# A two-block network on one core: conditioning weights by column blocks, four v tiles beside their load, later conditioning units spread

## The chip, the cores and the metric

The kernel runs on one core of a Trainium2 chip. The metric is the time of one execution on the device in microseconds; of several executions the median counts. The engines are TensorE (PE in the profile; PEld is its loading of stationary operands), VectorE (DVE), ScalarE (ACT), GpSimd (POOL) and SyncE (SP, which here only issues loads of weights).

## What is computed

Two blocks on 256 tokens of width D = 2048. The first has two layers, and each is steered by a conditioning vector: `mod = silu(cond) @ ada_w + ada_b`, three parts of 2048 each (shift, scale, gate).

```python
sh, sc, g = ada_params(c, ada_w[layer], ada_b[layer])     # latent; for the context with c_ctx
xm = x * (1.0 + sc) + sh
q, k, v, o, z_m, gates, u_p, z_p = split(xm @ w_in)       # layer 0, latent and context
x  = layer_norm(ALPHA * x + g * (y @ w_out), ln_g, ln_b)
```

Layer 0 is an mLSTM in both directions beside a pooling branch; it needs shift and scale for the latent and the context input, and k, v and gates for both. Layer 1 is a gated spatial mixer (u1, v1, z1) for the latent input alone. The second block (attention, a linear recurrence, an expert network) takes the rest of the time, and nothing of it is touched. `ada_w` has 2 x 3 parts of 2048 x 2048 float32.

## The kernel before

All weights come in **units** of 128 x 2048 float32 (1 MB) through a ring of RING = 4 slots in SBUF, in the order of the table STAGES: a name, a pattern of N and P, how often it is repeated, tiles per N unit, and the engine that takes the results out of PSUM. SP issues a load when its slot is free again (L364), strictly in that order.

An **N unit** is 16 weight blocks of 128 x 128. float32 products are made in three products of a faster format (fp32r): ScalarE copies each half of a unit into `unit_hi` (L862, two halves of 1024 columns), GpSimd makes the rest `unit_lo` = ring - unit_hi (L421), and TensorE multiplies hi x hi, hi x lo and lo x hi (L474, `n_unit`). The inputs have a hi and a lo as well. There are NBUF = 4 half-unit buffers: ScalarE may write a half when TensorE is done with the one four halves back (`half_done`), and a slot of the ring is free when `lo_done` says that both rests are made. A unit with one input set has 48 products of 256 columns, one with latent and context (gates, k, v) 96. Results go to four tiles of PSUM in turn; a tile is free again when `tile_free` has been counted up by VectorE or ScalarE.

A **P unit** is used as it is. `ada_ss`, 32 of them at the start, are rows of `ada_w` for shift and scale of layer 0: TensorE takes `cond` (128 x 2) as stationary operand and multiplies 4 x 512 columns per unit in plain float32 (L535), for all 16 parts of the contraction, so that no column is done before the last unit. Then the two rows are copied out (L1303, L930), turned into columns by 32 small products (L542), `mod` is made, VectorE makes the modulated inputs (L1314), ScalarE their hi (L883), GpSimd and VectorE their lo (L406, L1218), and gates can begin. The other 64 P units (gate of layer 0; shift, scale, gate of layer 1) are needed for one row only: VectorE multiplies each by its entry of `cond` and adds it to `ada_acc`, 128 x 2048 (`ada`, L1164). After each 16 of them TensorE sums over the partitions by 16 products of one column (`ada_sum`, L484). These P units stand among the N units: 16 in v, 16 in k, 4 each in q, o, zm and up, 16 in out0.

In v every result is copied to `vstage`, transposed (L554) and copied to `v` by VectorE (`v_step`, `v_out`). Between these steps VectorE does the chain of the gates (`log1p`, L1230 to L1238, and scans). In out0 and out1 VectorE adds each tile to the residual (L1549) and to `h_acc` (L1272); in v1 it copies it and adds it to `h_acc`.

## Time and profile before

| | us |
|---|---|
| median of 3 executions | 4313.85 (4307.5 to 4319.14) |
| the profiled execution | 4325.57 |
| its span, first to last instruction | 4323.8 |
| PE busy | 3878.8 (90%) |
| POOL busy | 3107.3 (72%) |
| DVE busy | 1800.1 (42%) |
| ACT busy | 1612.5 (37%) |

Busy times overlap. TensorE's records are pipelined, so its busy time is an upper bound of its work. The chain of work that ended last consists of PE for 73% of the span, DVE for 13%, POOL for 5% and time of issue for 6%. Its largest lines are L474 (49%) and L838 in the expert network (17%). All weights together are 671 loads of 1 MB.

### The profile page before, as it was taken

How to read it: one execution, taken by the hardware profiler on the slowest of the kernel's cores; microseconds unless marked ns; L12 is line 12 of the kernel's file. 1: busy time of each engine (PE TensorE's matmuls, PEld its weight loads, DVE VectorE, ACT ScalarE, POOL GpSimd, SP SyncE). 2: the span in 40 equal slices, each digit the busy share in tenths (PEclk: the TensorE clock that was granted, in tenths of full speed). 3: DMA queues.
4: the chain of work that ended last, by engine and by line, in shares of the span. 5: the costliest groups of instructions: out<-in, count | busy, mean ns of one | idle time of the engine just before them, and what ended most of it. 6: DMA issues, size and time to landing. Idle time of an engine off the chain costs nothing.

```text
span 4323.8 us, 78214 instructions
## 1 busy us (share of the span) xinstructions
PE 3878.8 (90%) x31142; PEld 3695.3 (85%) x31142; DVE 1800.1 (42%) x2279; ACT 1612.5 (37%) x2283; POOL 3107.3 (72%) x1292
## 2 busy tenths in 40 slices
PE   9699996879998889989998999948999999399987
PEld 1599995779997779989998999938999999399986
DVE  0667357845123351381133492194442000944433
ACT  0112432233343333354433344454443444544442
POOL 0357970867785647778887798878887888888864
PEclk9799997989998999999999999959999999599998
DMA  8367650734443323444444444504454544045532
GB/s 348 122 247 263 263 195 0 269 137 158 166 176 112 129 106 146 156 160 181 177 176 159 180 175 184 185 10 156 184 185 174 184 184 175 0 175 185 186 136 98
DMA packets 98367, 713.79 MB, mean 165 GB/s; under 512 B 11040, under 2 KB 11168, under 8 KB 12064
## 3 DMA queue, kind: packets, MB, share of 16 engines
q1 hardware_dynamic: 97344, 705.75, 43.7%
q10 hardware_dynamic: 864, 5.76, 0.4%
q8 instruction: 119, 1.95, 0.2%
q14 instruction: 40, 0.33, 0.0%
HBM read 709.37 MB, written 2.10 MB: 165 GB/s over the span
## 4 chain that ended last, share of the span: by engine, by line
PE 73%; DVE 13%; issue 6%; POOL 5%; ACT 2%; DMA 1%; DVEq 0%; POOLq 0%; ACTq 0%; SPq 0%
PE bank L474 49%; PE bank L838 17%; POOL unit_lo L421 5%; PE bank L535 2%; DVE hot L1856 1%; PE bank L521 1%; DMA ring<-in_w 1%; DVE peer_w L1870 1%; DVE log_a L1747 1%; DVE hot L1863 1%; DVE rms_tmp L1612 1%; PE bank L627 1%; PE bank L609 0%; DVE y_attn L1733 0%; ACT att_s L1010 0%
## 5 line engine op out<-in xcount | busy, mean ns | idle before, releaser
L421 POOL TENSOR_TENSOR unit_lo<-ring,unit_hi 128x1024 fp32r<-128x1024 f32 x1140 | 2867.9, 2532 | 872.2 <-ACT unit_hi L862 871.0
L474 PE MATMUL bank<-xl_hi,unit_hi 128*128 128x256 f32 x5696 | 1614.3, 283 | 144.0 <-POOL unit_lo L421 58.7
L862 ACT ACTIVATE unit_hi<-ring 128x1024 fp32r<-128x1024 f32 x1140 | 1173.3, 1055 | 1314.8 <-PE bank L474 522.3
L474 PE MATMUL bank<-xl_lo,unit_hi 128*128 128x256 f32 x5696 | 1604.0, 282 | 0.0
L474 PE MATMUL bank<-xl_hi,unit_lo 128*128 128x256 f32 x5696 | 1602.7, 281 | 0.0
L474 PEld LDWEIGHTS bank<-xl_hi,unit_hi 128*128 128x128 f32 x5696 | 1083.4, 190 | 158.6 <-issue 70.9
L474 PEld LDWEIGHTS bank<-xl_lo,unit_hi 128*128 128x128 f32 x5696 | 1082.9, 190 | 0.1
L474 PEld LDWEIGHTS bank<-xl_hi,unit_lo 128*128 128x128 f32 x5696 | 1082.8, 190 | 0.0
L838 PE MATMUL bank<-w_r,unit_hi 128*128 128x256 f32 x4096 | 727.8, 280 | 6.9 <-DVE w_r L1894 6.9
L838 PEld LDWEIGHTS bank<-w_r,unit_hi 128*128 128x128 f32 x4096 | 628.5, 189 | 7.2 <-issue 7.2
L838 PE MATMUL bank<-w_r,unit_lo 128*128 128x256 f32 x2048 | 573.1, 280 | 0.0
L1894 DVE TENSOR_TENSOR w_r<-peer_w,w_r 128x256 fp32r<-128x256 f32 x128 | 294.4, 2300 | 424.3 <-ACT w_r L1103 424.3
L838 PEld LDWEIGHTS bank<-w_r,unit_lo 128*128 128x128 f32 x2048 | 386.0, 188 | 0.0
L1856 DVE TENSOR_TENSOR hot<-con,peer_gT 128x512 bf16<-128x512 f32 x64 | 96.6, 1510 | 434.6 <-ACT hotg L1092 434.6
L1164 DVE SCALAR_TENSOR_TENSOR ada_acc<-ring,cond,ada_acc 128x2048 f32<-128x2048 f32 x64 | 214.5, 3351 | 69.5 <-DMA ring<-in_w 65.5
L439 POOL TENSOR_TENSOR hotg<-hot,gate_parts 128x512 bf16<-128x512 bf16 x128 | 189.2, 1500 | 52.5 <-DVE hot L1856 42.3
L815 PE MATMUL bank<-hotg,hot 128*128 128x64 bf16 x1536 | 91.7, 239 | 143.2 <-POOL hotg L439 136.9
L1079 ACT ACTIVATE peer_w<-bank 128x256 f32 (+1 forms) x128 | 49.3, 385 | 446.3 <-PE bank L474 446.3
L815 PEld LDWEIGHTS bank<-hotg,hot 128*128 128x128 bf16 x1536 | 83.3, 128 | 151.7 <-issue 151.7
L1092 ACT ACTIVATE hotg<-hot,peer_gT 128x64 bf16<-128x64 bf16 x512 | 128.5, 334 | 100.2 <-DVE hot L1856 100.2
L535 PE MATMUL bank<-ring,cond 128*2 128x512 f32 x256 | 112.5, 601 | 7.3 <-DMA ring<-in_w 7.2
L1863 DVE TENSOR_TENSOR hot<-con,peer_gT 128x1024 bf16<-128x1024 f32 x64 | 116.0, 1812 | 0.0
(362 smaller groups left out, 4333.0 us busy)
## 6 DMA issues: line engine op xcount, KB each, us to landing
ring<-in_w SPq DMA_DIRECT2D x671, 1024.0 KB, 4.8
resid<-in_xT ACTq DMA_DIRECT2D x1, 2048.0 KB, 12.8
tmp_ctx<-in_ctxT ACTq DMA_DIRECT2D x1, 2048.0 KB, 10.0
out<-resid SPq DMA_DIRECT2D x4, 512.0 KB, 2.6
con<-in_con ACTq DMA_DIRECT2D x1, 576.0 KB, 3.5
...
```

The source lines that it names most:

```text
L421: pool.tensor_tensor(lb[b][:], ring[slot][:, f * HALF:(f + 1) * HALF], hb[b][:].bitcast(F32), ALU.subtract).then_inc(lo_done, 1)
L439: ins = pool.tensor_tensor(ob[k][:, x], oe[k][:], gb[:, x, bass.ds(it * (2 * TG) + k * TG, TG)].unsqueeze(2) .to_broadcast([P, TG, I2]), A ...
L474: mm = pe.matmul(bank[(s.t0 + tile[m]) % TILES][:, 0:T], w[b][:, (i % 8) * P:(i % 8 + 1) * P], mv[x][:, k, :], start=(k == 0 and w is hb a ...
L535: mm = pe.matmul(bank[4 * (u % 2) + i][0:2, :], cond[:, u // 2, :], ring[u % RING][:, i * 512:(i + 1) * 512], start=(u < 2), stop=(u >= 2 ...
L815: mm = pe.matmul(bank[5 + k][:, t * I2:(t + 1) * I2], oa[k][:, t, :], ob[k][:, x, t, :], start=(x == 0), stop=(x == 2), skip_group_check=True)
L838: mm = pe.matmul(o, w_[b][:, c * P:(c + 1) * P], wr[j % 2][:, x, :], start=(first and j == 0 and cc % 2 == 0 and w_ is hb and x == 0), sto ...
L862: act.activation(hb[b][:], ring[slot][:, f * HALF:(f + 1) * HALF], ACT.Copy).then_inc(hi_done, 1)
L1092: ins = act.activation(ob[k][:, 0, t, :], oe[k][:, t, :], ACT.Copy, scale=gT[:, 2:3, bass.ds(it * (2 * TG) + (k * TG + t), 1)] .rearrange( ...
L1164: dve.scalar_tensor_tensor(a[:], ring[u % RING][:], col, a[:], ALU.mult, ALU.add).then_inc(plain_done, 1)
L1856: dve.tensor_tensor(oe[k][:], bc(C("iota", r * I2, (r + 1) * I2), TG), gT[:, 1, bass.ds(i * TG, TG)].unsqueeze(2).to_broadcast([P, TG, I2] ...
L1863: dve.tensor_tensor(oa[k][:], bc(C("iota"), TG), gT[:, 0, bass.ds(i * TG, TG)].unsqueeze(2) .to_broadcast([P, TG, NKEY]), ALU.is_equal).th ...
L1894: dve.tensor_tensor(wr[j % 2][:, 1, :], at(W, i), wr[j % 2][:, 0, :].bitcast(F32), ALU.subtract).then_inc(S("wr_ready"), 1)
```

## The change

- The load stage is renamed `first` and has 36 units, all N. 32 are A units: 4 parts of the contraction x 512 features of `ada_w`, shift or scale, so that the columns of one block of 512 are done after 8 units (g = 0 to 3). `cond` too is split in hi and lo, side by side as a stationary operand of 4 columns (`cond_parts`): one product with `unit_hi` gives cond_hi x hi and cond_lo x hi in separate rows, one with `unit_lo` gives cond_hi x lo (`ada_unit`). VectorE adds the two pairs of columns when it makes `mod` (`modulated`).
- Behind each g the rows are copied, turned (8 small products, `ada_turn`), and 4 chunks of the modulated inputs are made, hi by ScalarE, lo by VectorE (`x_hi`, `x_lo`).
- 4 are L units: the first four v tiles, one quarter g of the contraction each, for both inputs into four banks (`both_sets`). They stand at places 12, 21, 34 and 35 of the 36.
- In this stage VectorE makes the rests of the units; GpSimd waits until it is over.
- v keeps 4 N units and 8 P. gates go to a bank of their own. The transposes of the v tiles run through v and the first three k units.
- out0 has P after every second N (8 in all, the last two closer), v1 gets 8 P and z1 gets 8. There are six sums in place of four: after v, k, up, within out0, within u1 and after z1. The scale of layer 1 is now in v and out0, the gate of layer 1 in v1 and z1, and parts of `mod` are put together in two steps.

```diff
-    ("ada_ss", "PPPP", 8, 0, "D"),
+    ("first", "N" * 36, 1, 0, "D"),
     ("gates", "N", 1, 2, "D"),
-    ("v", "NPPNPPNPPNPP", 2, 2, "D"),
-    ("k", "NPPNPPNPPNPP", 2, 2, "D"),
+    ("v", "NPP" * 4, 1, 2, "D"),
+    ("k", "NPP" * 8, 1, 2, "D"),
     ("q", "NNPNNPNNPNNP", 1, 1, "D"),
     ("o", "NNPNNPNNPNNP", 1, 1, "A"),
     ("zm", "NNPNNPNNPNNP", 1, 1, "A"),
     ("up", "NNPNNPNNPNNP", 1, 1, "D"),
     ("zp", "NNNN", 2, 1, "A"),
     ("poolw", "P", 1, 0, "D"),
-    ("out0", "NPNPNPNP", 4, 1, "D"),
-    ("v1", "NNNN", 4, 1, "D"),
+    ("out0", "NNP" * 6 + "NPNPNN", 1, 1, "D"),
+    ("v1", "NNPNNPNNPNNP", 2, 1, "D"),
     ("u1", "NNNN", 4, 1, "A"),
     ("wsp", "P", 1, 0, "D"),
-    ("z1", "NNNN", 4, 1, "A"),
+    ("z1", "NNP" * 6 + "NPNPNN", 1, 1, "A"),
...
+FIRST = ([("A", 0, i) for i in range(8)] + [("A", 1, i) for i in range(4)] + [("L", 0, 0)]
+         + [("A", 1, i) for i in range(4, 8)] + [("A", 2, i) for i in range(4)] + [("L", 1, 0)]
+         + [("A", 2, i) for i in range(4, 8)] + [("A", 3, i) for i in range(8)] + [("L", 2, 0), ("L", 3, 0)])
+ENDS = [FIRST.index(("A", g, 7)) for g in range(4)]
...
+            pool.wait_ge(lo_done, 2 * NFIRST)
+            for s in ORDER[1:]:
...
-                pe.wait_ge(plain_done, PLAN["out0"].p0 + KC if b == 3 else 2 * KC + KC * (b + 1))
+                name, n = (("v", 8), ("k", 16), ("up", 4), ("out0", 8), ("v1", 8), ("z1", 8))[b]
+                pe.wait_ge(plain_done, PLAN[name].p0 + n)
+                a = accs.get(name, acc)
...
+            def ada_unit(n, g, i):
+                b = i // 4
+                rows = bank[4 + b]
+                if i % 4 == 0 and g:
+                    pe.wait_ge(S("ada_rows"), 2 * (g - 1) + b + 1)
+                for f in range(2):
+                    u = (2 * n + f) % NBUF
+                    pe.wait_ge(lo_done, 2 * n + f + 1)
+                    for q in range(2):
+                        k = 4 * (i % 4) + 2 * f + q
+                        pe.matmul(rows[0:4, :], ch[:, k, :], hb[u][:, q * 512:(q + 1) * 512],
+                                  start=(k == 0), stop=False, skip_group_check=True)
+                        mm = pe.matmul(rows[0:2, :], ch[:, k, 0:2], lb[u][:, q * 512:(q + 1) * 512],
+                                       start=False, stop=(k == KC - 1), skip_group_check=True)
+                    mm.then_inc(half_done, 1)
+            def ada_turn(g):
+                pe.wait_ge(S("ada_rows"), 2 * g + 2)
+                if g:
+                    pe.wait_ge(S("mod_ready"), g)
+                for b in range(2):
+                    for c in range(GR):
+                        mm = pe.matmul(bank[6][:, 4 * (b * GR + c):4 * (b * GR + c) + 4],
+                                       arow[:, b, c * P:(c + 1) * P], ident[0:4, 0:4],
+                                       start=True, stop=True, skip_group_check=True)
+                mm.then_inc(S("ada_cols"), 1)
...
+            for n, (kind, g, i) in enumerate(FIRST):
+                for gt_ in range(NG):
+                    if n == ENDS[gt_] + (2 if gt_ < 3 else 1):
+                        ada_turn(gt_)
+                if kind == "A":
+                    ada_unit(n, g, i)
+                    continue
+                pe.wait_ge(S("xm_lead"), 2 * g + 2)
+                for f in range(2):
+                    b = (2 * n + f) % NBUF
+                    pe.wait_ge(lo_done, 2 * n + f + 1)
+                    for i in range(8 * f, 8 * f + 8):
+                        mm = both_sets(bank[i % 4], (hb, lb), b, i, (xl, xc), GR * g + i // 4,
+                                       g == 0 and i < 4, g == 3 and i >= 12)
+                    mm.then_inc(half_done, 1)
...
+            v_transposes(0)
+            pe.wait_ge(S("v_lead"), 8)
+            run("v", [xl, xc], extra=lambda it, j: v_transposes(j + 1))
...
+            run("out0", [xl], extra=lambda it, j: ada_sum(3) if j == 14 else None)
             acc_sum(bank[5][:, 0:T], 1, "ln0_sum")
             feature_sum(sq0, bank[6][:, 0:T], "ln0_in", 1, "ln0_sum")
-            ada_sum(3)
...
+            run("u1", [xl], mid=(1, lambda: ada_sum(4)))
...
+            ada_sum(5)
...
+            def modulated(g):
+                dve.wait_ge(S("ada_cols"), g + 1)
+                if g == 0:
+                    dve.wait_ge(S("vec_in"), 16)
+                for b, first, one in ((0, 16, 1.0), (1, 0, 0.0)):
+                    cols = bank[6][:, 16 * b:16 * b + 16].rearrange("p (c s) -> p c s", s=4)
+                    part = mod[:, first + GR * g:first + GR * (g + 1), :]
+                    bias = V("ada_b", first + GR * g, GR).unsqueeze(2).to_broadcast([P, GR, 2])
+                    go(dve.scalar_tensor_tensor(part, cols[:, :, 0:2], one, bias, ALU.add, ALU.add)); sync()
+                    go(dve.tensor_tensor(part, cols[:, :, 2:4], part, ALU.add))
+                event("mod_ready")
+                for x, s, tmp, name in ((h, 0, tl_, "x_in"), (tc_, 1, tc_, "ctx_in")):
+                    if g == 0:
+                        dve.wait_ge(S(name), 16)
+                    for c in range(GR * g, GR * (g + 1)):
+                        go(dve.tensor_scalar(tmp[:, c, :], x[:, c, :], mcol(16 + c, s), mcol(c, s), ALU.mult, ALU.add))
+                    event("xm_tmp")
+            def x_lo(g):
+                for m, (pair, src) in enumerate(((xl, tl_), (xc, tc_))):
+                    lo([group(pair[0], g), group(pair[1], g)], group(src, g), "xm_hi", 2 * g + m + 1, "xm_lead")
+            for n in range(NFIRST + 1):
+                for g in range(NG):
+                    if n == ENDS[g] + (3 if g < 3 else 2):
+                        modulated(g)
+                    if n == ENDS[g] + (5 if g < 3 else 3):
+                        x_lo(g)
+                for f in range(2 if n < NFIRST else 0):
+                    b = (2 * n + f) % NBUF
+                    dve.wait_ge(hi_done, 2 * n + f + 1)
+                    dve.tensor_tensor(lb[b][:], ring[n % RING][:, f * HALF:(f + 1) * HALF], hb[b][:].bitcast(F32),
+                                      ALU.subtract).then_inc(lo_done, 1)
+            dve.wait_ge(half_done, NBUF + 2 * NFIRST)
+            dve.wait_ge(S("xm_lead"), 2 * NG)
...
+            dve.wait_ge(S("ada_sum"), 4)
+            go(dve.tensor_tensor(mod[:, 64:80, 0], bank[4][:, 112:128], mod[:, 64:80, 0], ALU.add)); sync()
+            go(dve.tensor_tensor(mod[:, 64:80, 1], mod[:, 64:80, 0], V("pln_g", 0, KC), ALU.mult))
+            go(dve.tensor_tensor(mod[:, 48:64, 1], mod[:, 64:80, 0], V("pln_b", 0, KC), ALU.mult)); sync()
+            go(dve.tensor_tensor(mod[:, 48:64, 1], mod[:, 48:64, 1], mod[:, 48:64, 0], ALU.add)); sync()
```

The order of VectorE in the load stage, before: behind a wait for all 32 units, the rows are copied (`ada_rows`), `mod` is made (L1307, L1309), and the first four chunks of the latent input follow.

```order
L1303 COPY ada_rows<-bank 2x512 x4
L1307 TENSOR_TENSOR mod<-bank,vec 128x64
L1309 TENSOR_SCALAR mod<-mod 128x32
L1314 TENSOR_SCALAR tmp_lat<-resid,mod 128x256 x4
L1288 MEMSET tick 1x1
L1314 TENSOR_SCALAR tmp_lat<-resid,mod 128x256 x4
```

Now, around the end of the first group of 8 A units: rests of two units, the four small instructions for `mod`, four chunks of each input, and again rests of units (`ring_49` to `ring_52` are the slots of the ring).

```order
L1419 TENSOR_TENSOR unit_lo_59<-ring_50,unit_hi_55 128x1024
L1419 TENSOR_TENSOR unit_lo_60<-ring_50,unit_hi_56 128x1024
L1396 SCALAR_TENSOR_TENSOR mod<-bank,vec 128x8
L1397 TENSOR_TENSOR mod<-bank,mod 128x8
L1396 SCALAR_TENSOR_TENSOR mod<-bank,vec 128x8
L1397 TENSOR_TENSOR mod<-bank,mod 128x8
L1371 MEMSET tick 1x1
L1403 TENSOR_SCALAR tmp_lat<-resid,mod 128x256 x4
L1371 MEMSET tick 1x1
L1403 TENSOR_SCALAR tmp_ctx<-tmp_ctx,mod 128x256 x4
L1371 MEMSET tick 1x1
L1419 TENSOR_TENSOR unit_lo_57<-ring_51,unit_hi_53 128x1024
```

What was one stretch with nothing else on the engine stands now, in four parts, in the stream of the rests for which TensorE waits.

VectorE in out0, before, two N units (the addition into the accumulator, the residual, the sum for LayerNorm):

```order
L1164 SCALAR_TENSOR_TENSOR ada_acc_107<-ring_52,cond,ada_acc_107 128x2048
...
L1549 SCALAR_TENSOR_TENSOR resid<-bank,mod,resid 128x256
...
L1272 TENSOR_TENSOR h_acc<-h_acc,resid 128x256
...
L1164 SCALAR_TENSOR_TENSOR ada_acc_107<-ring_50,cond,ada_acc_107 128x2048
...
L1549 SCALAR_TENSOR_TENSOR resid<-bank,mod,resid 128x256
...
L1272 TENSOR_TENSOR h_acc<-h_acc,resid 128x256
```

Now, three N units:

```order
L1655 SCALAR_TENSOR_TENSOR resid<-bank,mod,resid 128x256
L1355 TENSOR_TENSOR h_acc<-h_acc,resid 128x256
L1247 SCALAR_TENSOR_TENSOR ada_acc_108<-ring_49,cond,ada_acc_108 128x2048
L1655 SCALAR_TENSOR_TENSOR resid<-bank,mod,resid 128x256
L1355 TENSOR_TENSOR h_acc<-h_acc,resid 128x256
L1655 SCALAR_TENSOR_TENSOR resid<-bank,mod,resid 128x256
L1355 TENSOR_TENSOR h_acc<-h_acc,resid 128x256
L1247 SCALAR_TENSOR_TENSOR ada_acc_108<-ring_52,cond,ada_acc_108 128x2048
```

An addition of 128 x 2048 comes before every second unit and no longer before every one.

## Rows read from the trace of the kernel before

**Rows 1.** The page: span, and PEclk over 40 slices of 108 us.

```profile
span 4323.8 us, 78214 instructions
...
PEclk9799997989998999999999999959999999599998
```

**Rows 2.** Windows by stage: length, busy us of each engine (instructions), granted clock, DMA share, GB/s.

```profile
0.00:122.50 122.50, 112.51 (x256) 21.76 (x256) 4.47 (x12) 5.53 (x8) 4.86 (x6) 1.00 0.89 344
122.50:135.20 12.70, 12.66 (x64) 12.60 (x64) 0.00 (x0) 0.00 (x0) 0.00 (x0) 0.55 0.33 129
135.20:161.20 26.00, 0.00 (x0) 0.00 (x0) 23.98 (x43) 11.63 (x11) 13.13 (x5) 0.50 0.00 0
161.20:174.40 13.20, 13.14 (x96) 12.93 (x96) 0.00 (x0) 0.00 (x0) 4.53 (x2) 0.87 0.21 81
174.40:289.00 114.60, 104.42 (x849) 103.89 (x849) 86.83 (x75) 22.41 (x21) 57.63 (x18) 0.93 0.58 221
...
752.20:872.00 119.80, 96.51 (x768) 93.41 (x768) 97.22 (x59) 35.09 (x35) 102.85 (x32) 0.96 0.69 261
...
895.70:1018.90 123.20, 106.86 (x801) 104.08 (x802) 38.61 (x74) 45.58 (x41) 79.04 (x33) 0.91 0.37 137
```

**Rows 3.** Timeline of PE: start, us, instructions, [idle before and what ended it].

```profile
122.54 12.66 PE L542 MATMUL bank<-con,ada_rows 2*128 2x2 f32 x64 [2.73 <-DVE ada_rows L1303]
161.22 0.58 PE L474 MATMUL bank<-xl_hi,unit_hi 128*128 128x256 f32 x1 [26.02 <-DVE xc_lo L1218]
```

**Rows 4.** Lines, 0 to 1330 us: count | busy, mean ns | idle before.

```profile
L421 POOL TENSOR_TENSOR unit_lo<-ring,unit_hi 128x1024 fp32r<-128x1024 f32 x276 | 758.0, 2769 | 364.0 <-ACT unit_hi L862 363.6
...
L862 ACT ACTIVATE unit_hi<-ring 128x1024 fp32r<-128x1024 f32 x276 | 281.6, 1054 | 520.4 <-DMA ring<-in_w 372.7 <-PE bank L474 147.4
L1164 DVE SCALAR_TENSOR_TENSOR ada_acc<-ring,cond,ada_acc 128x2048 f32<-128x2048 f32 x64 | 214.5, 3351 | 69.5 <-DMA ring<-in_w 65.5 <-DVE ada_acc L1164 1.8 <-DVE ada_acc L1172 0.5
...
L484 PE MATMUL bank<-con,ada_acc 128*128 128x1 f32 x128 | 16.8, 265 | 0.0
```

**Rows 5.** Timeline of DVE, single rows from the load stage to v1.

```profile
137.24 1.38 DVE L1314 TENSOR_SCALAR tmp_lat<-resid,mod 128x256 f32<-128x256 f32 x4
...
191.79 0.76 DVE L1348 COPY vstage<-bank 128x256 f32<-128x256 f32 x2
192.46 4.81 DVE L1164 SCALAR_TENSOR_TENSOR ada_acc<-ring,cond,ada_acc 128x2048 f32<-128x2048 f32 x2
...
819.79 4.49 DVE L1164 SCALAR_TENSOR_TENSOR ada_acc<-ring,cond,ada_acc 128x2048 f32<-128x2048 f32 x1
...
824.79 2.00 DVE L1272 TENSOR_TENSOR h_acc<-h_acc,resid 128x256 f32<-128x256 f32 x1
...
904.22 2.36 DVE L1225 TENSOR_TENSOR xl_lo<-tmp_x,xl_hi 128x1024 fp32r<-128x1024 f32 x2
```

**Rows 6.** Timeline of ACT: the third v unit.

```profile
203.74 2.00 ACT L862 ACTIVATE unit_hi<-ring 128x1024 fp32r<-128x1024 f32 x2 [23.05 <-DMA ring<-in_w]
```

**Rows 7.** Windows: DMA while early units land.

```profile
25.00:30.00 5.00, 5.00 (x13) 1.00 (x12) 0.00 (x0) 0.00 (x0) 0.00 (x0) 1.00 1.03 426
```

**Rows 8.** Windows: o to up, out0, u1, after an L484 sum, first 3.4 us of gates.

```profile
441.23:575.06 133.83, 132.21 (x1107) 130.85 (x1107) 43.41 (x19) 54.28 (x64) 131.24 (x47) 1.00 0.71 271
...
810.40:866.00 55.60, 46.81 (x384) 45.21 (x384) 51.02 (x25) 16.06 (x16) 55.20 (x17) 1.00 0.79 302
...
1018.90:1109.70 90.80, 90.80 (x772) 90.77 (x771) 45.44 (x27) 36.73 (x48) 79.12 (x32) 1.00 0.46 174
...
284.20:289.00 4.80, 4.80 (x24) 4.77 (x24) 0.00 (x0) 2.24 (x1) 2.54 (x2) 0.50 0.00 0
...
161.20:164.60 3.40, 3.38 (x16) 3.38 (x17) 0.00 (x0) 0.00 (x0) 3.40 (x2) 0.50 0.02 5
```

**Rows 9.** Timelines: PE at the start of out1, POOL within out0.

```profile
1221.42 0.55 PE L474 MATMUL bank<-y_hi,unit_hi 128*128 128x256 f32 x1 [4.22 <-POOL y_lo L406]
...
799.11 48.21 POOL L421 TENSOR_TENSOR unit_lo<-ring,unit_hi 128x1024 fp32r<-128x1024 f32 x14 [0.56 <-ACT unit_hi L862]
```

More of the change, by code:

```diff
@@ L1320, in _ @@
+            dve.wait_ge(half_done, NBUF + 2 * NFIRST)
+            dve.wait_ge(S("xm_lead"), 2 * NG)
+            for t in range(4):
+                for m in range(2):
+                    dve.tensor_copy(vst[:, t, m, :], bank[t][:, m * T:(m + 1) * T]).then_inc(S("v_lead"), 1)
+            ada_start(0)
             s = PLAN["gates"]
@@ L1562, in _ @@
             event("h1_ready")
[L1563 to L1564 removed]
+            ada_start(4)
             acc_start()
```

206 lines of the change are left out of this document (109 added, 97 removed).

## The prediction

> **What bounds the kernel now.** The page first: the span is 4323.8 us, and PEclk is 9 in nearly every slice [rows 1], so TensorE sets the time almost everywhere, and what can be won lies in stretches where it waits. Then the windows by stage [rows 2]. The reader is to see three kinds. From 0 to 122.5 us TensorE is busy 112.5 us, but with the conditioning product alone, two useful rows wide. From 122.5 to 161.2 us it does 12.7 us of tiny transposes and then nothing for 26 us, because VectorE, ScalarE and GpSimd build the modulated inputs one after the other. From 161.2 us on it computes with all its columns: gates in 13.2 us, then v in 114.6 us of which 8 units need 8 x 11.3 = 91. The timeline of PE shows the empty 26.02 us, ended by the last rest of the context input [rows 3]. The last kind is out0: 119.8 us for 16 units [rows 2], though 16 units of u1 take 90.8 [rows 8]. There the timelines of VectorE and GpSimd are the ones to read [rows 5, 9].
>
> The executions shown have a median of 4313.85 us; the profiled one took 4325.57 (span 4323.8), 12 us more. I make the sum as a difference against the profiled times and take it from the median.
>
> **A. The load stage (0 to 161 us before).** Let F be the moment at which the new stage ends. It has 36 units of 1 MB in place of 32: 32 A units (conditioning, 512 columns) and 4 L units (four v tiles, a quarter of the contraction each).
> - TensorE, A unit: before, 128 products of 512 columns in float32 filled 112.5 us, 3.5 us a unit. Now a unit is 8 products of 512 columns in the split format. A 256-column product of that format takes 90.80 / 768 = 0.118 us in u1 [rows 8], so 512 columns take 0.235 and a unit 1.9 us. L unit: 96 products, 11.3 us. Turns: the same 32 small products, 12.66 / 32 = 0.40 each [rows 3], now 8 at a time, 3.2 us. Sum on TensorE: 61 + 45 + 13 = 119 us.
> - VectorE makes every rest: 72 instructions like the two at 904.22, 1.18 us each [rows 5], 85 us. It also makes, four times, 8 modulated chunks (two times the 1.38 of the row at 137.24), about 1 us of small ones and two rests: 6.2 us each, 25 us. Sum 110 us. ScalarE: 72 x 1.054 [rows 4] = 76 us, plus about 13.
> - DMA: 36 units and 5.3 MB of inputs and constants are 43 MB; at the 426 GB/s of [rows 7] 101 us.
>
> None of them alone gives F, since with four half-unit buffers they follow each other. Put in order: (1) start and first 8 A units, paced by DMA because the inputs come among them: 16 MB, 37 us, and 3 to start, 40 us; (2) the other 24 A units at VectorE's pace, 2.4 us: 57; (3) four L units on TensorE, 45, less what VectorE prepares beneath the first two, 2 x 4.7: 36; (4) the work beside it on VectorE, three times 6.2, the fourth lying beneath the third L unit: 19; (5) the wait for each turn, about 2 us, three times, and the last turn before the third L unit, 3: 9. That is 161 us. To this comes the clock. A units leave TensorE idle for a fifth to a half of the time. Where such gaps stood before, the granted clock went to 0.5: 0.50 in the 26 empty us [rows 2], and gates began at 0.50 for 3.4 us and took 13.1 us instead of 11.3 [rows 8, 2]. At that level an A unit costs 3.8 us instead of the 2.4 of the pace. I count 8 A units so (11 us): **F = 172**. Bounds: 161 with no loss; all 24 at half clock, 24 x 1.4 = 34, and each L unit with a cold start of 1.8, 7: 202.
>
> The rule that speaks against the change: the Trainium skill, "TensorE: Matmul & The Clock Gate", section "Loop structure matters more than you think", warns that a loop which waits for a DMA between its products lets TensorE go cold, so that each starts slow. By that rule F would be the 202 of the upper bound. For the opposite, the old load stage, with two stationary columns but no gaps, ran at 1.00 throughout [rows 2].
>
> The DMA rate of [rows 7] is 426 GB/s. The Trainium skill, "DMA: Bandwidth & Descriptors", gives about 358 GB/s as what a core gets from HBM; by it step (1) would take 7 us more, and the row decides.
>
> **B. Gates and v.** Gates follow at once, on a bank of their own: F + 11.3 = 183.3, against 174.4 before: **+9**. From there to the first k unit it was 114.6 us [rows 2]. Four of eight v units are gone, 45.3 us: **-45**. What stays: the gate chain on VectorE, up to the copy at 191.79 and the two weight additions behind it [rows 5], which free the ring slots of the third unit; ScalarE sees its weights at 203.74 only [rows 6], so they are ready near 208, while TensorE is through two units near 200. Now one more copy out of the transposes stands in that chain, twice: **+1**. VectorE was busy 86.83 us in this stretch [rows 2]; less 8 additions of 3.35 [rows 4] and three steps it is 57, and TensorE has 69 with its waits, so VectorE does not take over. k: three transposes move in: **+1**. Sum of A and B: -34.
>
> **C. out0.** Before, one P unit per N unit. VectorE's addition takes 2.4 alone, 4.49 when it meets GpSimd [rows 5], and GpSimd's rests come 14 in 48.21 us, 3.44 each, 6.9 us a unit [rows 9]; TensorE shows 55.6 / 8 = 6.95 [rows 8]. Now it is 8 P on 16 N. Two P in six units gave 133.83 / 23 = 5.82 in o to up [rows 8]; here two additions into h_acc come in, so 5.95. Before, 16 x 6.95 = 111, so 8.6 of the 119.8 went at the start, where TensorE waits for y0 and then for weights that stand behind a P still held by VectorE. With P every third place the second of these waits should go: 3.5 stay. 16 x 5.95 + 3.5 and 3 for the closing N P N P = 102, and the sum of the accumulator at the 15th unit, 16 products, 4.2 [rows 4], which keeps TensorE so thinly used that 0.50 follows [rows 8], 2 more: 108, **-12**. At the old pace it would be +6.
>
> **D. Later.** LayerNorm behind out0 now stands behind four small instructions, each of which can meet GpSimd at 2.1 us (4.49 - 2.4): **+2** (1 to 8). v1 gets 8 P: 16 x 0.2: **+3** (0 to 20, the upper one if it took out0's old pace). A fifth sum stands in u1, where nothing covers it: 4.2 and 2.5 for the clock: **+6.5**. z1 gets 8 P with an idle VectorE: **+1.5**. The sixth sum fits in the 4.22 us in which TensorE waits before out1 [rows 9]: 0; if the wait were gone, +4. The other small waits: **+1**. Sum +14. The P that left v cost nothing there after step B.
>
> **Sum.** 9 - 45 + 1 + 1 - 12 + 14 = -32. 4313.85 - 32 = **4282 us**. One measurement of this kernel tells about 0.3%, 13 us, from no change; that is 4301 to 4327.
>
> **The rivals.**
> 1. *Clock low throughout A units.* F = 202 in place of 172, -2 in all: 4312. For it: the clock stood at 0.50 in and behind the 26 us gap [rows 2, 8]. Against: the gaps here are about 1 us, and at the low level an A unit (3.8 us) fills its own gaps, which raises the clock again.
> 2. *Slower than before: L units at half clock too.* Each L unit then takes 22.6 us instead of 11.3: 45 us on top of 202, F about 245, 73 more than forecast: 4355. It decides for slower by 0.3% from F = 217 on. Against it: gates, as dense as an L unit, began at 0.50 [rows 8] but had 0.87 over its 13.2 us [rows 2], so the rest ran near full clock.
> 3. *Spreading pays nothing.* out0 keeps its GpSimd pace or v1 and z1 take it over: C and D give +20 instead of +2: 4300. For it: GpSimd is busy in 55.20 of 55.60 us in out0 [rows 8], and P instructions are what slows it.
> 4. *Load stage as tight as its sums.* F = 155 and 3 less in out0: 4262. For it: VectorE's 110 us leave room. Against it: the buffers hold two units only.
> 5. *The change doesn't do what it says:* VectorE, not v, sets the start of k. If its 86.83 us of that stretch stay, only 26 of the 45 come: 4301. Against it: half of its 16 additions there are gone.
>
> **How the numbers follow.** Forecast 4282: 0.56 (F from 161 to 182, 4268 to 4294). Rival 1: 0.15, a third of it, where it is only partly so, under 4301. Rival 2: 0.04. Rival 3: 0.09, half of it under 4301. Rival 4: 0.13. Rival 5: 0.03. The range leaves out rival 2, half of rival 1 and a little beyond rival 4: **4258 to 4308**. Faster by over 0.3%: 0.56 + 0.13 + 0.05 + 0.05 + 0.02 = 0.81. Slower: rival 2 and a little of rival 1, 0.05. Within 0.3%: the remaining 0.14.
>
> **What would show it.** The last L unit should end at 165 to 180 us, k begin at 245 to 260 (289 before), the product of an A unit last 1.9 us at full clock and VectorE's rests 1.1 to 1.2 us. In out0 TensorE should show 5.8 to 6.0 us a unit, in v1 under 6. The prediction is wrong if the granted clock up to F is under 0.8, if VectorE's rests take much more than 1.2 us, if two A units take over 6 us where DMA is idle, or if v1 or z1 give back what out0 gains.

## The result and the profile after

The changed kernel takes **4278.3 us** (median of 4 executions, 4275.9 to 4279.3), beside 4316.5 us for the kernel before in the same session: a ratio of **0.991, interval 0.989 to 0.993**. The forecast was 4282 us, 0.993 of the 4313.85 known then. The profiled execution has a span of 4277.0 us, 46.8 less than before.

The clock over 40 slices, from the page, and windows by stage; they answer to [rows 1] and [rows 2].

```profile
PEclk9999998899999999999999999959999999599998
```

Columns: stretch, length, busy us (instructions) of PE, PEld, DVE, ACT and POOL, granted clock, DMA share, GB/s.

```profile
0.00:43.00 43.00, 22.12 (x73) 6.02 (x73) 22.93 (x28) 23.21 (x26) 0.20 (x4) 0.96 0.95 395
43.00:140.50 97.50, 83.85 (x442) 44.77 (x441) 76.18 (x102) 60.36 (x64) 0.00 (x0) 0.91 0.73 278
140.50:176.20 35.70, 35.70 (x291) 35.70 (x291) 12.66 (x28) 7.64 (x7) 9.60 (x4) 0.95 0.37 140
176.20:241.70 65.50, 56.75 (x454) 56.27 (x451) 54.16 (x56) 13.53 (x13) 30.62 (x10) 0.91 0.50 193
704.90:810.90 106.00, 99.32 (x800) 97.31 (x800) 75.81 (x49) 35.80 (x35) 97.69 (x33) 0.97 0.62 239
834.50:947.00 112.50, 97.50 (x768) 95.84 (x768) 82.62 (x75) 39.40 (x36) 93.38 (x33) 0.93 0.54 206
962.40:1060.00 97.60, 97.60 (x805) 97.56 (x804) 32.81 (x27) 36.76 (x49) 78.03 (x32) 0.97 0.44 162
1076.90:1174.50 97.60, 92.50 (x774) 91.21 (x772) 40.58 (x23) 34.52 (x46) 86.43 (x30) 1.00 0.70 270
```

The rows are: the first nine conditioning (A) units, up to the first turn; the other 23 with the four turns and two units of v weights (L) among them; the last two L units with gates; v with its sum and the gate columns; out0, v1, u1, z1. The 26 empty microseconds of [rows 3] are gone. Gates end at 176.2 us (174.4 before) and k begins at 241.7 (289.0 before): **-47.3**. out0 takes 106.0 in place of 119.8: -13.8. What is given back lies behind it. The end of out1 is this row of PE's timeline, of the kernel before and then of the changed one:

```profile
1316.08 0.70 PE L527 MATMUL bank<-h_acc,con 128*128 128x256 f32 x2 [1.47 <-DVE tick L1288]
```

```profile
1274.24 0.70 PE L544 MATMUL bank<-h_acc,con 128*128 128x256 f32 x2 [1.38 <-DVE tick L1371]
```

1274.24 against 1316.08 is -41.8, so of 61 us gained 19 have gone again by then: v1 and the LayerNorm behind it 4.7, u1 6.8, z1 6.8, the rest around them. The other 5 of the 46.8 lie in the untouched part behind out1, where two executions of one kernel differ by as much (3002.8 us here, 2996.2 in the second trace of the changed kernel). That is why the verdicts below go by marks in the trace, and by timed medians only where these can tell.

Five readings, four inside the load stage and one in v. A group of instructions by line (count | busy us, mean ns | idle before, and what ended it), then PE's timeline:

```profile
L1419 DVE TENSOR_TENSOR unit_lo<-ring,unit_hi 128x1024 fp32r<-128x1024 f32 x72 | 84.0, 1221 | 34.8 <-ACT unit_hi L928 34.5
```

```profile
16.45 0.59 PE L560 MATMUL bank<-unit_hi,cond_parts 128*4 128x512 f32 x1 [16.45 <-DMA con<-in_con]
...
42.98 1.94 PE L574 MATMUL bank<-con,ada_rows 4*128 4x4 f32 x16
...
50.09 0.59 PE L560 MATMUL bank<-unit_hi,cond_parts 128*4 128x512 f32 x1 [3.22 <-DVE unit_lo L1419]
...
209.13 0.58 PE L489 MATMUL bank<-xl_hi,unit_hi 128*128 128x256 f32 x1 [7.07 <-POOL unit_lo L436]
```

VectorE makes the 72 rests at 1.22 us each and stands idle ahead of them for 34.8 us in all. TensorE begins only at 16.45 us, because it waits for the constants, which nothing reads before the first turn. A turn takes 1.94 us. One A unit behind it TensorE stands for 3.22 us, since VectorE makes the modulated chunks before the next rests. And ahead of the third v unit it waits 7.07 us.

### The profile page after: what moved, and what is told of

The parts are those of the page before. It is cut to its first block, busy times and chain, and to the rows that moved or that the text cites. A ratio compares the mean times of both kernels' runs of the same rounds, so it can differ in the third digit from the quotient of the medians.

```text
span 4277.0 us, 77792 instructions
## 1 busy us (share of the span) xinstructions
PE 3837.9 (90%) x31206; PEld 3689.9 (86%) x31206; DVE 1897.7 (44%) x2379; ACT 1678.5 (39%) x2352; POOL 3091.8 (72%) x1280
## 4 chain that ended last, share of the span: by engine, by line
PE 66%; DVE 14%; POOL 10%; issue 6%; ACT 2%; DMA 1%; DVEq 0%; POOLq 0%; ACTq 0%; SPq 0%
PE bank L489 43%; PE bank L904 17%; POOL unit_lo L436 10%; DVE hot L1975 1%; PE bank L583 1%; DMA ring<-in_w 1%; PE bank L538 1%; DVE peer_w L1989 1%; DVE log_a L1866 1%; DVE hot L1982 1%; DVE unit_lo L1419 1%; DVE rms_tmp L1731 1%; PE bank L692 1%; ACT unit_hi L928 1%; PE bank L674 0%
## 5 line engine op out<-in xcount | busy, mean ns | idle before, releaser
L928 ACT ACTIVATE unit_hi<-ring 128x1024 fp32r<-128x1024 f32 x1204 | 1237.6, 1055 | 1206.4 <-PE bank L489 525.0
L489 PE MATMUL bank<-xl_hi,unit_hi 128*128 128x256 f32 x5616 | 1590.7, 283 | 112.8 <-POOL unit_lo L436 48.8
L489 PE MATMUL bank<-xl_hi,unit_lo 128*128 128x256 f32 x5616 | 1580.9, 282 | 0.0
L489 PE MATMUL bank<-xl_lo,unit_hi 128*128 128x256 f32 x5616 | 1579.7, 281 | 0.0
L489 PEld LDWEIGHTS bank<-xl_hi,unit_hi 128*128 128x128 f32 x5616 | 1066.7, 190 | 128.6 <-issue 74.1
L489 PEld LDWEIGHTS bank<-xl_lo,unit_hi 128*128 128x128 f32 x5616 | 1068.3, 190 | 0.1
L489 PEld LDWEIGHTS bank<-xl_hi,unit_lo 128*128 128x128 f32 x5616 | 1068.0, 190 | 0.0
L1247 DVE SCALAR_TENSOR_TENSOR ada_acc<-ring,cond,ada_acc 128x2048 f32<-128x2048 f32 x64 | 226.7, 3542 | 83.6 <-DMA ring<-in_w 82.0
L1419 DVE TENSOR_TENSOR unit_lo<-ring,unit_hi 128x1024 fp32r<-128x1024 f32 x72 | 84.0, 1221 | 34.8 <-ACT unit_hi L928 34.5
```

The source lines that it names most:

```text
L489: mm = pe.matmul(bank[(s.t0 + tile[m]) % TILES][:, 0:T], w[b][:, (i % 8) * P:(i % 8 + 1) * P], mv[x][:, k, :], start=(k == 0 and w is hb a ...
L928: act.activation(hb[b][:], ring[slot][:, f * HALF:(f + 1) * HALF], ACT.Copy).then_inc(hi_done, 1)
L1247: dve.scalar_tensor_tensor(a[:], ring[u % RING][:], col, a[:], ALU.mult, ALU.add).then_inc(plain_done, 1)
L1419: dve.tensor_tensor(lb[b][:], ring[n % RING][:, f * HALF:(f + 1) * HALF], hb[b][:].bitcast(F32), ALU.subtract).then_inc(lo_done, 1)
```

## The experiments

Each mark is one row of PE's timeline: the first product of v, whose time counts from the kernel's start. It stands 2.1 us behind the last product of the gates: 0.6 us of transposes, partly beneath it, and 1.68 us of waiting. The changed kernel was run again beside the first three; its row is the base:

> The changed kernel itself once more, on the chip of the three runs beside it, so that they are compared with a run of the same chip. Every theory expects 0.991 of the kernel before and, in its trace, the last product of the load stage at 165 us, k beginning near 242 us, out0 106 us, v1 112.5 us, u1 and z1 97.5 us each.

```profile
177.59 0.36 PE L489 MATMUL bank<-xl_hi,unit_hi 128*128 128x256 f32 x1 [1.68 <-issue]
```

Measured: 4271.9 us, ratio 0.9895 (0.987 to 0.992). Base marks: v at 177.6, k at 241.7, out0 106.1, z1 97.

How far does such a mark move by itself? The load stage of the changed kernel was traced three times: v stands at 178.3 us in the first trace, at 177.6 in this one, and at 180.2 in the kernel of "Behind out0", which leaves this stage alone and ran on another chip. The first turn stands at 43.0, 42.7 and 43.6. So one trace doesn't show a difference of less than about 2.6 us at v. The stretch from out0's start to out1's end is steadier: 569.3 and 568.8 us in the first two. The timed medians of the kernels that change one thing in the changed kernel lie between 4265.7 and 4282.0 us; none of them tells such a change from none.

### The spreading alone

```diff
-    ("out0", "NPNPNPNP", 4, 1, "D"), ("v1", "NNNN", 4, 1, "D"),
+    ("out0", "NNP" * 6 + "NPNPNN", 1, 1, "D"), ("v1", "NNPNNPNNPNNP", 2, 1, "D"),
-            ada_sum(3)      # ahead of v1
-            run("u1", [xl])
+            run("u1", [xl], mid=(1, lambda: ada_sum(3)))
```

> The kernel before with the spreading alone: out0 has 8 weight additions on its 16 units in place of 16, v1 has the other 8, the sum of this part stands in u1. Load stage, v and z1 are those before. Theory (out0 was set by GpSimd meeting two VectorE additions a unit, and v1 has room): out0 from 119.8 to about 104 us (106 in the changed kernel less the 3.6 of the sum that stands inside it), v1 +3, the sum +6.7 in u1 in place of 4.2 ahead of v1; in all 4 to 10 us less than before, ratio 0.9977 to 0.999. Rival (out0 was 14 us quicker in the changed kernel because v no longer left it a queue of late weights, not because of the pattern): out0 stays at 115 to 120 us and the time rises by 3 to 8 us. Second rival (the load stage brought everything): the time is that of before within 2 us.

Windows of out0, LayerNorm excluded, of v1 with its LayerNorm, of u1 with the gating, and of z1:

```profile
753.80:853.00 99.20, 92.98 (x756) 91.55 (x756) 73.21 (x45) 32.20 (x32) 90.63 (x32) 0.98 0.64 243
875.90:1002.40 126.50, 109.03 (x803) 105.22 (x803) 86.95 (x81) 45.03 (x41) 93.41 (x33) 0.88 0.53 200
1002.40:1115.00 112.60, 110.01 (x898) 106.65 (x897) 47.10 (x62) 40.40 (x52) 83.36 (x34) 0.98 0.38 141
1115.00:1209.90 94.90, 90.72 (x771) 90.51 (x769) 8.96 (x17) 38.53 (x51) 74.47 (x32) 1.00 0.54 197
```

out0 takes 99.2 us, not 119.8, while v is as before: the pattern did it, and v's queue had no part in it. v1 with its LayerNorm takes 3.3 more than the 123.2 of [rows 2], u1 with the gating 5, where the sum stands. By the end of out1 11 us are left, just over the 4 to 10 expected. The timed ratio is 0.9986 (0.9967 to 1.0005): it agrees, but alone it would not tell 11 us from none. This kernel also splits what the changed one does later: there out0 takes 106.1, 7 more, of which 3.9 are the sum inside it; z1 with the wait behind it 101.1 in place of 94.9.

### The order of the long units

```diff
-FIRST = ([("A", 0, i) for i in range(8)] + [("A", 1, i) for i in range(4)] + [("L", 0, 0)]
-         + [("A", 1, i) for i in range(4, 8)] + [("A", 2, i) for i in range(4)] + [("L", 1, 0)]
-         + [("A", 2, i) for i in range(4, 8)] + [("A", 3, i) for i in range(8)] + [("L", 2, 0), ("L", 3, 0)])
+FIRST = [("A", g, i) for g in range(4) for i in range(8)] + [("L", g, 0) for g in range(4)]
```

> The changed kernel, with the four units of v weights behind all 32 conditioning units in place of beside them. Theory (DMA, ScalarE and VectorE do the next units' work beneath an 11.5 us unit, but only as far as the buffers hold: four half units, 4 to 5 us of VectorE each): the load stage ends 5 to 10 us later, at 170 to 175 us, and the whole takes 5 to 10 us more. Rival 1 (the long units hide the load itself, as the change's words say: 23 us of TensorE disappear beside DMA): the stage ends about 20 us later. Rival 2 (order is free, since VectorE's work has the same sum in both): within 2 us of the changed kernel.

```profile
181.01 0.35 PE L487 MATMUL bank<-xl_hi,unit_hi 128*128 128x256 f32 x1 [1.68 <-issue]
```

The window of L0 in the changed kernel:

```profile
57.00:68.00 11.00, 11.00 (x96) 11.00 (x95) 4.15 (x4) 1.39 (x2) 0.00 (x0) 1.00 0.53 206
```

+3.4 us: neither my 5 to 10 nor the 20 of rival 1, and just over rival 2, whose 2 us the spread of the mark allows. Having the first two L units beside the load of the others, as the title has it, is worth some 3 us at most. While an L unit runs, VectorE works 4.15 of 11 us, as far as four half-unit buffers hold, and the DMA share is 0.53. That overlap makes the five A units behind it quicker: they take 10.5 us, near the 9.4 of TensorE alone (40 products of 0.235 us), and no more is won.

### The late start of TensorE

```diff
-            pe.wait_ge(S("con_in"), 16)          # ahead of the first unit
+                else: pe.wait_ge(S("con_in"), 16)    # in ada_turn, g == 0
```

> The changed kernel, with TensorE's wait for the constants moved from ahead of the first conditioning unit (where it holds TensorE until 16.4 us) to ahead of the first turn, which is the first that reads them. Theory A (TensorE's late start is made up, because the units come at the pace of DMA, so the four half buffers and four ring slots fill meanwhile and TensorE is quicker than the rest): the eighth unit ends at most 2 us earlier and the whole is within 3 us of the changed kernel. Theory B (the late start leaves the ring full and DMA idle, which is not made up): the stage ends 5 to 8 us earlier, and the whole takes as much less.

```profile
8.86 0.59 PE L560 MATMUL bank<-unit_hi,cond_parts 128*4 128x512 f32 x1 [8.86 <-DVE unit_lo L1420]
...
175.84 0.35 PE L489 MATMUL bank<-xl_hi,unit_hi 128*128 128x256 f32 x1 [1.68 <-issue]
```

TensorE starts 7.6 us earlier, the first turn 0.3 earlier, v 1.8 earlier, which is within the spread of the mark: theory A. The first 43 us are DMA's: share 0.95, 395 GB/s.

### Which engine sets the pace

One small instruction more per half unit on one engine at a time: a memset of 256 columns on VectorE, a 512-column product on TensorE (conditioning units only), a copy of 256 columns on ScalarE. All three write what nothing reads. Each of these kernels and of the next one was executed once, on a chip on which the base was not run.

> The changed kernel, with one more memset of 256 columns on VectorE ahead of each of the 72 rests of the load stage (with its wait about 0.25 us each, 18 us in sum). Theory V (VectorE sets the pace of this stage, except behind the long units, where TensorE does): the stage ends 9 to 16 us later, over half of what is added. Theory D (DMA sets it, as in the first 43 us, where its share is 1.0): under 3 us. Theory C (half-unit buffers chain the engines, so that what any engine adds shows nearly in full): as V here, and the same share in the two runs beside it.

> The changed kernel, with one more 512-column product into a bank that nothing reads, in each of the 64 halves of the conditioning units (0.235 us each, 15 us in sum). Theory V: 3 to 7 us later, since TensorE paces only the five units behind each long one and in between fills idle time. Theory D: under 3 us. Theory C: 10 us or more. The clock rival: with fewer idle gaps the granted clock rises and gives back some of it.

> The changed kernel, with one more copy of 256 columns on ScalarE ahead of each of the 72 rounded halves of the load stage (about 0.35 us each, 25 us in sum). Theory V: under 5 us later, as ScalarE rests a quarter of the stage. Theory D: under 3 us. Theory C: 15 us or more.

```profile
L1423 DVE MEMSET pad<- 128x256 f32 x72 | 19.6, 272 | 0.2
```

```profile
188.91 0.36 PE L490 MATMUL bank<-xl_hi,unit_hi 128*128 128x256 f32 x1 [1.67 <-issue]
```

```profile
181.84 0.36 PE L489 MATMUL bank<-xl_hi,unit_hi 128*128 128x256 f32 x1 [1.68 <-issue]
```

```profile
L931 ACT ACTIVATE pad<-ring 128x256 f32<-128x256 f32 x72 | 29.0, 403 | 33.4 <-PE bank L584 16.5 <-DMA ring<-in_w 9.6 <-PE bank L563 7.2
...
183.86 0.36 PE L490 MATMUL bank<-xl_hi,unit_hi 128*128 128x256 f32 x1 [1.67 <-issue]
```

| added on | us added | v later by | share |
|---|---|---|---|
| VectorE | 19.6 | 11.3 | 0.58 |
| TensorE | 64 x 0.235 = 15.0 | 4.3 | 0.28 |
| ScalarE | 29.0 | 6.3 | 0.22 |

VectorE sets most of the pace: its 11.3 us are far beyond the spread of 2.6. DMA's rival (none over 3 us) and the chained buffers' (the same share everywhere) both fall. The other two shares are too close to the spread to rank TensorE against ScalarE. Counted from the first turn, v came after 145.4, 138.0 and 140.1 us, against 134.9 to 136.6 in the three traces of the stage as it is. By the first turn VectorE's addition showed with 0.8 us only, as DMA sets the time there. ScalarE gave 1.3 us more than I allowed; 2.0 of its 6.3 stand in one place, ahead of the last turn, where TensorE waits 2.69 us for the copied rows in place of 0.68. Part of VectorE's 11.3 is the clock's: L1 took 13.1 us in place of 11.5, and the last two L units with gates 36.9 in place of 35.7. With TensorE's addition the granted clock was 0.98 between the first and the last turn, against 0.91 and 0.95 in the first two traces of the changed kernel: the clock rival has the direction right.

### Relief for VectorE from GpSimd

```diff
-                lo([group(pair[0], g), group(pair[1], g)], group(src, g), "xm_hi", 2 * g + m + 1, "xm_lead")
+                    pool.tensor_tensor(lo, src, hi, ALU.subtract).then_inc(S("xm_lead"), 1)
```

> The changed kernel, with the eight rests of the inputs in the load stage on GpSimd (idle there) in place of VectorE, where they take 1.22 us each, 9.8 us in sum. Theory V: the stage ends 3 to 8 us earlier, and k begins as much earlier; GpSimd's rests take near 2 us where VectorE is beside them. Theory D: no difference over 2 us. Rival P (the two engines disturb each other: VectorE's rests beside GpSimd's take 2 us and more in place of 1.22): 0 to 3 us later.

VectorE's and GpSimd's timelines from the first group of inputs on, then the group by line, then the mark:

```profile
49.26 6.46 DVE L1419 TENSOR_TENSOR unit_lo<-ring,unit_hi 128x1024 fp32r<-128x1024 f32 x2
```

```profile
48.87 2.46 POOL L427 TENSOR_TENSOR xl_lo<-tmp_lat,xl_hi 128x1024 fp32r<-128x1024 f32 x1 [48.41 <-ACT xl_hi L1004]
51.29 3.34 POOL L427 TENSOR_TENSOR xc_lo<-tmp_ctx,xc_hi 128x1024 fp32r<-128x1024 f32 x1
```

```profile
L1419 DVE TENSOR_TENSOR unit_lo<-ring,unit_hi 128x1024 fp32r<-128x1024 f32 x72 | 100.2, 1448 | 38.9 <-ACT unit_hi L934 38.6
```

```profile
186.88 0.36 PE L495 MATMUL bank<-xl_hi,unit_hi 128*128 128x256 f32 x1 [1.67 <-issue]
```

Eight rests (9.8 us) left VectorE, and the stage ends **9.3 us later**, beyond even rival P. Two rests beside GpSimd's two take 6.46 us in place of 2.4 (two of 1.22), and the 72 together 16.4 more. TensorE waits for them: ahead of the first L unit 5.27 and 1.44 us for `unit_lo`, where the base has 3.23 and 1.86. Behind the longer wait its products run at half the clock, 20 of them 0.43 us apart, and L0 starts at 60.60, about 1.4 us after the rest it needs: that part is the clock's. The Trainium skill, "SBUF — State Buffer", section "Who interferes with whom", says that a VectorE instruction with two inputs in SBUF contends with a GpSimd instruction that reads SBUF, and that the later one is blocked, not slowed. These rows agree: 6.46 is the two rests and about 4 us of waiting. So GpSimd, idle in this stage, is no spare room for it. What the units' own rests would cost on GpSimd, as the kernel before has them, no run shows.

### The inputs in groups

```diff
-                    act.dma_start(h[:], A["xT"]).then_inc(S("x_in"), 16)
+                if n in (2, 9, 18, 25):      # four groups of features
+                    act.dma_start(group(h, g), A["xT"][:, g * GR:(g + 1) * GR, :])
```

> The changed kernel, with x and the context loaded in four groups of features: the first group among the first units, the others beside units 9, 18 and 25; TensorE's wait for the constants stands ahead of the first turn. Theory D1 (the first 43 us are set by DMA, whose share is 1.01 there, and 3 MB of the inputs aren't needed in them: 3 MB at 423 GB/s are 7.4 us): the first turn begins 5 to 8 us earlier, VectorE's pace holds behind it, and the stage ends 5 to 8 us earlier. Rival D2 (the bytes only move to where the units need them, and DMA is late there): the first turn comes earlier but the stage ends within 2 us of before. Rival V (VectorE's sums alone set the end): within 2 us, with the first turn no earlier.

```profile
0.00:34.90 34.90, 20.63 (x73) 5.47 (x73) 22.54 (x27) 22.80 (x25) 0.20 (x4) 1.00 0.95 386
34.90:134.60 99.70, 82.91 (x442) 45.31 (x441) 76.68 (x103) 60.75 (x65) 0.00 (x0) 0.92 0.82 316
```

```profile
172.87 0.36 PE L489 MATMUL bank<-xl_hi,unit_hi 128*128 128x256 f32 x1 [1.68 <-issue]
```

The first turn comes 7.8 us earlier (theory D1), v 4.7, a little under its 5 to 8. Against the trace of the same chip, that of "Behind out0", it is 8.8 and 7.4. The second stretch took 97.1 us and takes 99.7, at a DMA share of 0.82 in place of 0.74. So a part of D2 is true too: the moved bytes cost some 3 us where they went. The edit also moves the wait for the constants, as the run above (0.3 at the first turn, 1.8 at v); its part in the 4.7 is not separated.

### The wait ahead of the third v unit

```diff
-... ("L", 2, 0), ("L", 3, 0)]   # gates behind
+... ("L", 2, 0), ("G", 3, 0)]   # the last L behind gates
+            log1p(gw[:], gt[:], gp[:], gq[:], lead_out)   # copies of the four tiles between two of its steps
```

> The changed kernel, with the gates' unit ahead of the last unit of v weights in place of behind it; VectorE takes the gates' chain up beneath that unit, copies the four v tiles between two of its steps, and does the first two weight additions of v ahead of the first v step. Theory G (TensorE's wait of 7.1 us ahead of the third unit of v comes of the chain on VectorE, which holds the additions and with them the ring slots): that wait goes to under 1 us and k begins 6 to 9 us earlier. Rival R (the wait is the load's own, as the unit stands behind four P in a ring of four): 5 to 7 us of it stay. Rival S (slower: the copies of the four tiles now wait behind the chain's steps): v's first unit starts 2 to 4 us later and k at most 4 us earlier.

PE's timeline at the start of v and at its fourth unit:

```profile
183.40 1.12 PE L625 MATMUL bank<-con,vstage 128*128 128x128 f32 x4 [5.61 <-DVE vstage L1463]
185.38 0.58 PE L489 MATMUL bank<-xl_hi,unit_hi 128*128 128x256 f32 x1 [0.87 <-DVE vstage L1463]
...
224.40 0.38 PE L489 MATMUL bank<-xl_hi,unit_hi 128*128 128x256 f32 x1 [1.90 <-POOL unit_lo L436]
```

The 7.07 us are gone, but 5.61 + 0.87 + 1.90 = 8.4 came in their place, as the copies stood behind the chain: k begins at 244.2, and counted from the last turn's end (139.8 there, 142.1 here) nothing is gained. That is rival S, only stronger: v's first unit starts 7.8 us later, of which 2.3 lie ahead of the last turn, where the two kernels are the same. VectorE's timeline suggested why the wait exists: the first two additions of v stood at 191.8 to 196.6, and the ring could not go on before them, though their weights had landed long before. The last experiment tests it.

### Behind out0

```diff
+            acc_sum(bank[5][:, 0:T], 1, "ln0_sum")
+            ada_sum(3)                       # was inside out0; ada_sum(4) likewise behind v1, was in u1
+    ("v1", "NPNNPNNPNNPN", 2, 1, "D")        # no P behind the last N
```

> The changed kernel with three things moved behind out0: the fourth and fifth sum stand between the two sums of the LayerNorm behind out0 and v1 (with VectorE's small scale instructions beneath the second one) in place of inside out0 and u1; v1's weights for addition stand one place earlier, so that none follows its last unit; out0 and z1 have an even pattern to the end. Theory T (each sum inside a stage costs its 3.6 us and 1 to 3 for the clock behind it, in the LayerNorm only what is over the 2.5 us in which TensorE waits anyway): out0 -4 to -5, u1 -5 to -6.5, the two LayerNorms +1.2 each, the wait at v1's end from 3.8 to 1.5, z1 -1 to -2; in all 8 to 12 us less than the changed kernel. Rival (the sum delays the second sum of the LayerNorm, and VectorE's small instructions get between it and the root): LayerNorms +4 each, in all 2 to 4 us less.

Windows of out0, v1 with LayerNorm, u1 with gating, z1; first of the changed kernel, then of this one:

```profile
701.60:807.70 106.10, 101.04 (x800) 99.38 (x800) 75.01 (x48) 35.90 (x35) 97.67 (x33) 0.94 0.63 238
831.10:960.60 129.50, 107.61 (x802) 103.55 (x803) 90.63 (x82) 44.93 (x41) 95.49 (x33) 0.90 0.52 195
960.60:1073.50 112.90, 110.31 (x898) 106.94 (x897) 47.37 (x62) 40.37 (x52) 83.17 (x34) 0.98 0.40 140
1073.50:1174.60 101.10, 95.22 (x804) 93.74 (x802) 44.79 (x26) 38.67 (x51) 89.64 (x32) 1.00 0.70 268
```

```profile
707.20:808.00 100.80, 95.65 (x768) 93.61 (x768) 72.82 (x48) 35.79 (x35) 96.44 (x33) 0.97 0.63 237
833.70:964.00 130.30, 114.06 (x833) 110.73 (x834) 89.50 (x82) 45.26 (x41) 93.93 (x33) 0.87 0.52 194
964.00:1071.80 107.80, 105.20 (x865) 101.82 (x864) 59.95 (x62) 40.39 (x52) 84.35 (x34) 1.00 0.42 146
1071.80:1172.50 100.70, 96.20 (x803) 94.89 (x802) 44.48 (x26) 38.51 (x51) 90.54 (x32) 0.99 0.70 269
```

out0 -5.3, the LayerNorm behind it +2.3 (+1.2 expected), v1 with its LayerNorm +0.8, u1 -5.1, z1 -0.4; with what lies between, 8.7 us less from out0's start to out1's end: theory T in the lower part of its range. The timed ratio, 0.9904 (0.988 to 0.993), cannot show 9 us. The even pattern did nothing for z1, and the reason is in GpSimd's rests, first without P units in z1 (the kernel with the spreading alone), then with eight (the changed kernel):

```profile
L421 POOL TENSOR_TENSOR unit_lo<-ring,unit_hi 128x1024 fp32r<-128x1024 f32 x30 | 71.7, 2413 | 29.0 <-ACT unit_hi L862 29.0
```

```profile
L436 POOL TENSOR_TENSOR unit_lo<-ring,unit_hi 128x1024 fp32r<-128x1024 f32 x28 | 82.2, 2971 | 19.8 <-ACT unit_hi L928 19.8
```

2.97 us each, 5.94 a unit, where TensorE needs 5.67. TensorE waits for `unit_lo` five times there, 5.1 us in all, and not once without the P units: GpSimd sets z1's pace now.

### All of it, and v's additions early

The inputs in groups, the moves behind out0, and for v:

```diff
+            ada_start(0)
+            ada(PLAN["v"], 0, 0)        # right behind the last rests of the load stage
             dve.wait_ge(half_done, NBUF + 2 * NFIRST)
...
             v_out(0)
+            ada(sv, 1, 0)
             dve.wait_ge(S("gate_exp"), 1)
```

> The changed kernel with the inputs in four groups (as in inputs_split), the three moves behind out0 (as in tail) and, new here, the first four weight additions of v earlier: two of them right behind the last rests of the load stage, where VectorE waits 16 us for TensorE and their weights have landed, two behind the copies that free the four v tiles. In gates_early the wait ahead of the third v unit moved but did not go, and the loads of v stood from 167.8 to 196.2 us because the first two additions ended at 196. Theory E (those additions hold the ring, and so the third unit's weights): the wait of 7.1 us ahead of the third unit goes to under 1, and none comes ahead of the fourth; gates' end to k's begin takes 59 us in place of 66. With the load stage 4 to 5 us shorter k begins at 228 to 232 us (241.8 in the changed kernel), and with the moves behind out0, which gave 8.7 us, the kernel takes 19 to 21 us less than the changed one: a ratio of 0.984 to 0.987 to the kernel before. Rival R (the wait has another cause, the ring's order of four P ahead of the unit): 5 us or more of it stay, and the ratio is 0.986 to 0.989. Rival O (gains of single moves do not add up, since VectorE works at the end of the load stage already): less than 12 us under the changed kernel.

VectorE's timeline, then PE's:

```profile
145.16 5.73 DVE L1254 SCALAR_TENSOR_TENSOR ada_acc<-ring,cond,ada_acc 128x2048 f32<-128x2048 f32 x2
...
181.44 2.62 DVE L1320 TENSOR_SCALAR gate_t<-gate_w 64x512 f32<-64x512 f32 x1
...
197.97 0.76 DVE L1463 COPY vstage<-bank 128x256 f32<-128x256 f32 x2
```

```profile
172.88 0.36 PE L489 MATMUL bank<-xl_hi,unit_hi 128*128 128x256 f32 x1 [1.60 <-issue]
...
199.47 0.63 PE L623 MATMUL bank<-con,vstage 128*128 128x128 f32 x4 [3.71 <-DVE v L1454]
```

**4260.0 us** (4246.1 to 4265.8), ratio **0.9868 (0.985 to 0.988)**, beside 0.9895 (0.987 to 0.992) for the base. The ratio lies in theory E's range, but the two intervals touch, and by the medians the gain over the changed kernel is about 12 us, at the edge of rival O. In the trace k begins at 232.3, 9.5 earlier than in the base, and out1 ends 21 us earlier; the traced execution is the quickest of the four, 13.8 us under their median, so the 21 may flatter it. The weights of the first two additions are there at 145, and the third unit's come in time, so the additions did hold the ring. But a wait of 3.7 takes its place: the transposes stand behind VectorE's copies at 198, at the end of the gate chain, which the two early additions (6.75 us beside GpSimd) push back. Gates' end to k takes 61.5 us, against 66.3 in the base and the 59 of theory E: it has the cause right and promised 2.5 us too much there.

## Why the prediction was right, and where not

**A, the load stage.** Forecast F = 172, measured 164.7 (gates' end 176.2 less 11.5). Step (1), start and eight A units, was right: the ninth starts at 39.98 us, for 40. For steps (2) to (5) I had 121 us, and 124.7 came: 60.4 for 24 A units, 2.52 each (2.4 forecast), 47.0 for the four L units, 7.6 for the turns and 9.7 for the three waits behind turns. The **11 us for the clock** are the term that failed. The granted clock did fall to one half again and again, as behind the first turn, in the first trace and then in the second:

```profile
43.00:57.00 14.00, 10.42 (x42) 4.23 (x41) 12.76 (x24) 7.95 (x9) 0.00 (x0) 0.76 0.81 317
```

```profile
42.70:57.00 14.30, 9.21 (x44) 4.27 (x44) 13.66 (x25) 10.48 (x12) 0.00 (x0) 0.88 0.85 337
```

But the pace is VectorE's. In the first trace 14 products behind the wait came 0.43 us apart, at 1.2 GHz, in the second only 6; yet from the first turn to L0's first product it took 14.02 and 14.01 us, as TensorE only waited 0.35 us in place of 1.86 for the next rest. An A unit at 1.2 GHz (8 x 0.43 = 3.4 us) exceeds VectorE's 2.4 only for a unit or two at a time. The mean stayed at 0.91 to 0.96. In an L unit, which TensorE fills, the low clock does cost: from 141.3 to 144.7 us, in L2, it was 0.50, and 19 products ran where 29 would at 0.118 us each, 1.2 us. The rule of the Trainium skill that I weighed ("TensorE: Matmul & The Clock Gate", section "Loop structure matters more than you think") would have given 202; its gaps are here, 0.35 to 3.50 us, and of its price these 1.2 us. So of rival 1 little came, and of rival 2 no more: L0 and L1 took 11.4 us each, L2 and L3 24.2 together. Rival 4 (155) was the nearer one on the other side. No run tells the column blocks from the other two things that this stage changed, the split format of its products and the rests on VectorE.

**B.** From gates' end to k I forecast 71.6 us and 65.5 came, 49.1 less than the 114.6 of [rows 2]. Four units gave 45.3; the forecast +1 for the chain did not come, the transposes in k (+0.9) fell inside k, and the rest are small waits at v's start and end. The cause named for the wait at the third unit was right, as the last experiment shows: it stayed, at 7.07.

**C.** Right: 106.0 for 108, and the pattern is the cause, as the spreading alone shows.

**D.** +14 forecast, +19 measured. u1 +6.7 against +6.5, the sixth sum 0 as said, v1 +2.9. The failed term is **z1 +1.5**: it was 6.8. I took VectorE for idle there and asked only whether it had time for 8 P; they are slow for GpSimd, whose rests go from 2413 to 2971 ns, and GpSimd was near the bound. [Rows 8] had a part of it: o to up, with a P on every second unit, took 5.82 a unit where u1 took 5.67, 2.4 us in 16 units, with GpSimd busy in 131.24 of 133.83 us; why z1 takes 6.1 a unit and not 5.8 stays open. The four instructions ahead of the LayerNorm (+2) cost nothing: they ran from 811.98 to 812.66 us, while TensorE made the sum for which VectorE waits at that place anyway.

So 4282 was right to 4 us, while in the trace the -32 stand against -41.8: A and B 13 too dear, C 2, D 5 too cheap. That the number is this close is in part luck: errors of opposite sign cancel, and the median of one kernel moves by some microseconds from session to session (4278.3 and 4271.9 for this one). Two of the signs set beforehand came out on the quick side, the last L unit at 164.7 (165 to 180) and k at 241.7 (245 to 260), and z1 gave back half of what out0 gained. The new load stage with the shorter v gives 47 us. Spreading out0's units gives 11 net, and the eight units that left v cost 13.6 behind it: 7.4 in out0 and its LayerNorm, 6.2 in z1, by the two kernels that differ in them.
